# Two token halves of 320 in a diffusion step: PSUM slots by half, panels A A B B around norms, w_ada loaded with a later panel

## The chip, the cores and the metric
The kernel runs on one core of a Trainium2 chip. The metric is device time in microseconds (us) of one execution of the whole program. TensorE (PE) multiplies, VectorE (DVE) and ScalarE (ACT) work on vectors, GpSimd (POOL) helps with some of the weights, and SyncE (SP) issues the weight transfers.

## The reference
Two layers of a hybrid backbone run over 128 context and 512 latent tokens of width 1024, together 640 tokens with the same weights. The core of a layer is:

```python
n = rmsnorm(h, norm_g[l, 0]) * (1 + sc0) + s0
h = h + 0.5 * g0 * swiglu(n, w_ffn_up[l, 0], w_ffn_down[l, 0])
n = rmsnorm(h, norm_g[l, 1]) * (1 + sc1) + s1
y, ckv, k_r = token_mix(n, ...)
h = h + g1 * y
n = rmsnorm(h, norm_g[l, 2]) * (1 + sc2) + s2
h = h + 0.5 * g2 * swiglu(n, w_ffn_up[l, 1], w_ffn_down[l, 1])
```

All nine modulation vectors (s, sc, g) of a layer are c @ w_ada + b_ada: context and latent tokens have vectors of their own. The hidden width of swiglu is 2816. token_mix is one input product, a long convolution, attention, a Fourier mix, three gated branches and an output product. After the last layer comes a final rmsnorm.

## The kernel before
**Data.** Activations lie transposed: h is [128, 8, 640], eight blocks of 128 channels with all 640 tokens beside each other. A float32 product is made of three products of rounded halves: weights hi times input hi, hi times lo, and lo times hi. The tokens are cut into two halves of TH = 320. The second half has 192 latent and 128 context tokens; since modulation differs between the two kinds, an operation with a per-channel scalar is two instructions there.

**Panels.** Weights come as panels of 1 MB (two output tiles of 128 columns by 8 blocks of 128 rows; the last down projections of an FFN have 6 blocks). Each layer has 34 panels for an FFN (up 8, down 4, up 8, down 4, up 6, down 4), then 6 mix, 10 table, 4 head, 16 gate and 4 output panels, and again 34. There are SLOTS = 3 buffers. SP loads a panel into raw when PE has finished the panel three before it (`freed`), ACT rounds it to whi (round_panel, L734), DVE subtracts to wlo (split_panel, L1034). Both do so for the panel two ahead of the one PE is on, at a fixed place in their orders.

**PE.** `gemm` (L345) makes one output tile of all 640 tokens: it takes one of the two PSUM slots of tile_psum (two banks, one per half), runs 8 blocks x 2 inputs x 2 halves with whi (L355) and then 8 blocks x 2 halves with wlo (L360). A slot may be taken again when ACT or DVE has counted it free. An up panel holds a gate tile and an up tile.

**FFN on the other engines.** ACT applies Silu to the gate tile (L789), DVE multiplies it with the up tile (hidden, L1176), ACT rounds it (x_hi, L793), DVE makes x_lo (L1059). For a down panel DVE adds each tile into h (L1153); in the last chunk ACT squares h and DVE sums the squares.

**Norm.** When all of h is updated, PE sums the squares per token with ten small matmuls (L385), ACT takes the root, DVE the reciprocal and a diagonal of it (L1072), PE spreads it over the partitions (L389, L390), and DVE and ACT make n_hi and n_lo block by block (L1083, L771, L1098). PE starts the next stage's first tile as blocks come.

**w_ada.** 144 tiles of 512 KB are multiplied with the conditioning rows by DVE, two instructions each (L1118, L1120), inside `ada_step`, which stands behind each split_panel and takes as many tiles as ADA_PLAN says for the panel. 16 are done at the start. The rest have two buffers; DVE waits for a tile's transfer, SP's ada_load waits until DVE has used the tile two before. SP issues, in order, a panel load and then the w_ada tiles of the plan for the panel before it.

Every engine runs a fixed order written out in the program; the sequences of the listed functions are the order of work.

## Time and profile of the kernel before
| | us |
|---|---|
| median of 3 runs (lowest, highest) | 3858.5 (3857.25, 3859.94) |
| the profiled execution | 3861.88 |
| its span | 3860.1 |

| engine | busy us | share of the span |
|---|---|---|
| PE matmul | 3313.1 | 86% |
| PE weight load | 3140.2 | 81% |
| DVE | 1846.2 | 48% |
| ACT | 920.4 | 24% |
| POOL | 137.7 | 4% |

The mean granted clock of TensorE is 0.91 of 2.4 GHz. The core's transfers move 86 GB/s in the mean. Busy shares are means over stages. A wait is told with the engine and line that ended it; times in the timeline are from the start of the span. "L355" is line 355 of the kernel.

### The profile page before, as it was taken

The page shows a single profiled execution, that of the slowest core. Times are in us where ns is not written, and L with a number is a line of the kernel's source. Part 1 is how long each engine was busy: PE and PEld are TensorE (multiplying, and loading weights), DVE is VectorE, ACT ScalarE, POOL GpSimd, SP SyncE. Part 2 cuts the span into 40 slices and gives each one's busy share as a digit, 9 for nine tenths or more (in the row PEclk, how much of TensorE's full clock was granted, in tenths as well). Part 3 has the DMA queues.
Part 4 walks back from the last instruction along what each step waited for, and adds up shares of the span by engine and source line. Part 5 has one row for each costly group of instructions (what it writes and reads, how often), then busy time and mean ns, then how long its engine had stood idle before and what let it go on. Part 6 is the DMA issues. An engine that isn't in the chain of part 4 may idle for free.

```text
span 3860.1 us, 46383 instructions
## 1 busy us (share of the span) xinstructions
PE 3313.1 (86%) x20238; PEld 3140.2 (81%) x20238; DVE 1846.2 (48%) x2770; ACT 920.4 (24%) x1153; POOL 137.7 (4%) x100
## 2 busy tenths in 40 slices
PE   2998987766769998999979989796677799799998
PEld 2998987545659997999979989693466699799998
DVE  6445555567552244433454455646765333523223
ACT  2211112223331122111222111222233212321211
POOL 0000000221000000000000000001300000000000
PEclk9999998878779998999989999897876899899999
DMA  5333333110002122232323333230100222112221
GB/s 204 112 107 131 131 125 119 55 44 31 22 33 94 71 101 76 84 114 93 104 82 115 115 131 131 99 121 25 60 17 21 77 76 77 66 66 77 77 77 61
DMA packets 56891, 330.38 MB, mean 86 GB/s; under 512 B 6320, under 2 KB 6640, under 8 KB 29808
## 3 DMA queue, kind: packets, MB, share of 16 engines
q1 hardware_dynamic: 53280, 297.82, 21.6%
q10 hardware_dynamic: 3408, 29.60, 1.9%
q8 instruction: 159, 2.61, 0.3%
q14 instruction: 44, 0.36, 0.0%
HBM read 313.07 MB, written 14.32 MB: 85 GB/s over the span
## 4 chain that ended last, share of the span: by engine, by line
PE 66%; DVE 18%; DMA 6%; ACT 5%; issue 4%; SPq 0%; DVEq 0%; ACTq 0%
PE tile_psum L355 37%; PE tile_psum L360 19%; PE tile_psum L323 3%; DMA raw<-in_w_up 3%; PE misc_psum L530 2%; DVE scaled L1118 2%; ACT whi L734 2%; DVE wlo L1034 2%; DMA raw<-in_w_down 1%; PE misc_psum L323 1%; DVE w_ada L1120 1%; DVE n_lo L1098 1%; PE misc_psum L494 1%; DVE probs_t_lo L1059 1%; DMA n_lo<-n_keep 1%
## 5 line engine op out<-in xcount | busy, mean ns | idle before, releaser
L355 PE MATMUL tile_psum<-n_hi,whi 128*128 128x320 f32 x4224 | 990.1, 316 | 86.1 <-DVE n_lo L1098 38.9
L355 PE MATMUL tile_psum<-n_lo,whi 128*128 128x320 f32 x4224 | 980.6, 314 | 0.0
L355 PEld LDWEIGHTS tile_psum<-n_hi,whi 128*128 128x128 f32 x4224 | 718.9, 192 | 107.7 <-issue 63.2
L734 ACT ACTIVATE whi<-raw 128x2048 fp32r<-128x2048 f32 (+2 forms) x216 | 398.8, 1847 | 1466.7 <-PE tile_psum L360 945.4
L355 PEld LDWEIGHTS tile_psum<-n_lo,whi 128*128 128x128 f32 x4224 | 724.3, 192 | 0.0
L360 PE MATMUL tile_psum<-n_hi,wlo 128*128 128x320 f32 x4224 | 670.9, 311 | 0.0
L360 PEld LDWEIGHTS tile_psum<-n_hi,wlo 128*128 128x128 f32 x4224 | 639.9, 191 | 0.0
L1034 DVE TENSOR_TENSOR wlo<-raw,whi 128x2048 fp32r<-128x2048 f32 (+1 forms) x188 | 421.3, 2241 | 288.8 <-ACT whi L734 288.6
L355 PE MATMUL tile_psum<-x_hi,whi 128*128 128x320 f32 x1664 | 386.9, 314 | 59.4 <-DVE x_lo L1059 47.8
L355 PE MATMUL tile_psum<-x_lo,whi 128*128 128x320 f32 x1664 | 384.6, 313 | 0.0
L355 PEld LDWEIGHTS tile_psum<-x_hi,whi 128*128 128x128 f32 x1664 | 283.7, 192 | 62.7 <-DVE x_lo L1059 49.3
L1176 DVE TENSOR_TENSOR hidden<-gate_act,tile_psum 128x640 f32<-128x640 f32 x88 | 72.2, 820 | 477.1 <-PE tile_psum L360 475.1
L355 PEld LDWEIGHTS tile_psum<-x_lo,whi 128*128 128x128 f32 x1664 | 284.1, 192 | 0.0
L360 PE MATMUL tile_psum<-x_hi,wlo 128*128 128x320 f32 x1664 | 272.7, 313 | 0.0
L360 PEld LDWEIGHTS tile_psum<-x_hi,wlo 128*128 128x128 f32 x1664 | 255.5, 192 | 0.0
L717 POOL TENSOR_TENSOR wlo<-raw,whi 128x512 fp32r<-128x512 f32 x96 | 137.5, 1462 | 2760.1 <-ACT whi L734 2760.1
L1153 DVE SCALAR_TENSOR_TENSOR h<-tile_psum,ada_t,h 128x320 f32<-128x320 f32 x336 | 126.9, 433 | 205.9 <-PE tile_psum L360 204.5
L1059 DVE TENSOR_TENSOR x_lo<-hidden,x_hi 128x640 fp32r<-128x640 f32 x88 | 72.6, 825 | 308.3 <-ACT x_hi L793 308.3
L1118 DVE SCALAR_TENSOR_TENSOR scaled<-w_ada,c_rows 128x1024 f32<-128x1024 f32 x128 | 156.1, 1219 | 0.3
L1120 DVE SCALAR_TENSOR_TENSOR w_ada<-w_ada,c_rows 128x1024 f32<-128x1024 f32 x128 | 156.1, 1220 | 0.0
L789 ACT ACTIVATE gate_act<-tile_psum 128x640 f32<-128x640 f32 x88 | 61.7, 701 | 298.6 <-PE tile_psum L360 298.5
L1064 DVE TENSOR_TENSOR sq_sum<-sq_sum,squares 128x640 f32<-128x640 f32 x56 | 46.0, 822 | 139.0 <-ACT squares L754 139.0
(232 smaller groups left out, 2863.3 us busy)
## 6 DMA issues: line engine op xcount, KB each, us to landing
raw<-in_w_up SPq DMA_DIRECT2D x88, 1024.0 KB, 4.8
w_ada<-in_w_ada SPq DMA_DIRECT2D x128, 512.0 KB, 3.4
raw<-in_w_down SPq DMA_DIRECT2D x32, 1024.0 KB, 4.9
raw<-in_w_gate SPq DMA_DIRECT2D x32, 1024.0 KB, 4.8
raw<-in_tables SPq DMA_DIRECT2D x20, 1024.0 KB, 4.8
raw<-in_w_down SPq DMA_DIRECT2D x16, 768.0 KB, 4.4
raw<-in_w_mix SPq DMA_DIRECT2D x12, 1024.0 KB, 4.9
w_ada_early<-in_w_ada SPq DMA_DIRECT2D x16, 512.0 KB, 19.5
```

The lines of the kernel that those rows point to most:

```text
L323: ins = pe.matmul(o, w[a], x_[b], start=first and n == 0, stop=last and n == 2)
L355: pe.matmul(tps[:, t.s, j, 0:TH], blk(p, b0 + k)[0], x_[b], start=k == 0 and b == 0, stop=False)
L360: ins = pe.matmul(tps[:, t.s, j, 0:TH], blk(p, b0 + k)[1], x_[0], start=False, stop=k == n - 1)
L530: ins = pe.matmul(out, w[:, s, t * 512 + f * P:t * 512 + (f + 1) * P], x_[:, t, col:col + 512], start=b == 0 and t == 0 and x_ is tmh, sto ...
L717: ins = pool.tensor_tensor(wlo[:, s, a:b], raw[:, s, a:b], whi[:, s, a:b].bitcast(F32), ALU.subtract)
L734: act.activation(whi[:, r, 0:cols], raw[:, r, 0:cols], ACT.Copy).then_inc(hi_ready, 1)
L1034: dve.tensor_tensor(wlo[:, r, 0:cols], raw[:, r, 0:cols], whi[:, r, 0:cols].bitcast(F32), ALU.subtract)\
L1059: dve.tensor_tensor(out, src, hi.bitcast(F32), ALU.subtract).then_inc(ready, 1)
L1118: dve.scalar_tensor_tensor(out=junk, in0=w, scalar=1.0, in1=cb[:, 0, :], op0=ALU.mult, op1=ALU.mult, accum_out=ada[:, t, 0:1]).then_inc(ad ...
L1120: dve.scalar_tensor_tensor(out=w, in0=w, scalar=1.0, in1=cb[:, 1, :], op0=ALU.mult, op1=ALU.mult, accum_out=ada[:, t, 1:2]).then_inc(ada_u ...
L1153: ins = dve.scalar_tensor_tensor(out=hs, in0=tps[:, t.s, bank, c0:c1], scalar=ada[:, l * ADA_TILES + 8 * section + m, g:g + 1], in1=hs, op ...
L1176: dve.tensor_tensor(halves(hf[:, i % 2, :]), halves(sg[:, i % 2, :]), tile2(t), ALU.mult).then_inc(t.free, 1)
```

## The change
Each PSUM slot now holds the two output tiles of a panel (banks m = 0, 1) for one half of the tokens. `pair` (in place of `gemm` in the FFNs, the first two mix panels and the output panels) makes the (panel i, half j) unit; `walk` gives the order of units: for each panel half A then half B, but in the first two panels after a norm and the last two before it both A units and then both B units. A panel is freed by its B unit. `turn_of` gives the units behind which ACT and DVE round and split the next panel and DVE takes its w_ada tiles: the A unit of each panel (the B unit of the second panel behind a norm).

A norm is done per half. PE's sums for half A stand in the middle of the second last unit of the stage (token_sums(0)), its spread behind it, now as a product of the broadcast reciprocal with the identity, without DVE's diagonal. Half B's stand in the first unit of the next stage. DVE and ACT make five blocks of half A behind unit (n-2, B) and three behind the last unit; half B in two lots of four around the next stage's first unit.

ADA_PLAN is a list with one number per panel. SP's load of panel p waits for panel p-3, issues the panel, and then the w_ada tiles of the plan for panel p-3. Before, they were those of the plan for panel p-1. The output is stored in 16 pieces rather than 8, by half.

The diff, cut to its core. Removed lines of the functions printed above are left out in the engines' parts:

```diff
@@ -68,6 +68,8 @@
 SM_C, SM_S, SM_CI, SM_SI, SM_BD, SM_FC, SM_FS, NSM = 0, 128, 256, 384, 512, 768, 896, 1024
+HALVES = [[(0, TH, 0)], [(TH, TL, 0), (TL, T, 1)]]
+TOKEN_COLS = [(0, 0), (P, 0), (TH - P, TH - 2 * P)]
 SEGMENTS = [(0, 0, TH, 0, TH, 0), (1, 0, TL - TH, TH, TL, 0), (1, TL - TH, TH, TL, T, 1)]
...
 WIDTH = {"heads": 7 * P, "down6": 12 * P}
 ADA_EARLY = 16
-ADA_PLAN = [{"up0": 1, "down0": 1, "up1": 2, "down1": 2, "up2": 2, "down2": 1},
-            {"up0": 1, "down0": 0, "up1": 1, "down1": 0, "up2": 1, "down2": 1}]
+ADA_PLAN = [[0, 0, 2, 2, 1, 1, 1, 1] + [1] * 4 + [2] * 8 + [1] * 4 + [2] * 6 + [2, 2, 0, 0],
+            [0, 0, 2, 2, 1, 1, 1, 1] + [0] * 4 + [1] * 8 + [0] * 4 + [1] * 6 + [1, 1, 0, 0]]
+ADA_STEP = (ADA_PLAN[0] + [0] * (len(LAYER_KINDS) - 2 * len(FFN_KINDS)) + ADA_PLAN[1]) * DEPTH
+def walk(n, first=False, last=False):
+    steps = [(i, j) for i in range(n) for j in range(2)]
+    if first:
+        steps[:4] = [(0, 0), (1, 0), (0, 1), (1, 1)]
+    if last:
+        steps[-4:] = [(n - 2, 0), (n - 1, 0), (n - 2, 1), (n - 1, 1)]
+    return steps
+def turn_of(n, first=False, last=False):
+    return [(i, 1 if first and i == 1 else 0) for i in range(n - last)]
...
@@ tensor engine @@
+            held, norms_open = {}, {}
+            def pair(i, j, n, hi, lo, each=None, mid=None):
+                if j == 0:
+                    held[i] = panel_hi()
+                p = held[i]
+                t = taken(slots.tile())
+                tok = slice(j * TH, (j + 1) * TH)
+                for k in range(n):
+                    if each is not None:
+                        pe.wait_ge(*each(k))
+                    for b in range(2):
+                        for m in range(2):
+                            pe.matmul(tps[:, t.s, m, 0:TH], blk(p, m * n + k)[0], (hi, lo)[b][:, k, tok], start=k == 0 and b == 0, stop=False)
+                if j == 0:
+                    panel_lo(p)
+                if mid is not None:
+                    mid()
+                for k in range(n):
+                    for m in range(2):
+                        ins = pe.matmul(tps[:, t.s, m, 0:TH], blk(p, m * n + k)[1], hi[:, k, tok], start=False, stop=k == n - 1)
+                ins.then_inc(t.done, 1)
+                if j == 1:
+                    freed[p] = (t.done, t.done_at)
+            def token_sums(j):
+                norms_open[j] = m = taken(slots.misc())
                 pe.wait_ge(sum_ready, due(sum_ready))
+                for c, (a, _) in enumerate(TOKEN_COLS):
+                    ins = pe.matmul(mps[:, m.s, 0, 2 * c:2 * c + 2], acc[:, j * TH + a:j * TH + a + P], ones[:, 0:2], start=True, stop=True)
+                ins.then_inc(sums_done, 1)
+            def spread(j):
+                m = norms_open[j]
+                pe.wait_ge(inv_ready, due(inv_ready))
+                for c, (a, skip) in enumerate(TOKEN_COLS):
+                    ins = pe.matmul(mps[:, m.s, 1, a + skip:a + P], rr[:, 3 * j + c:3 * j + c + 1].broadcast_to([P, P]),
+                                    ident[:, skip:P], start=True, stop=True)
+                ins.then_inc(m.done, 1)
+            def from_norm():
+                now = due.now(n_ready)
+                due(n_ready, 2 * KT)
+                return lambda j: lambda k: (n_ready, now + KT * j + k + 1)
+            def begin(steps, coming, opened, n, hi, lo):
+                for i, j in steps[:4]:
+                    late = (i, j) == (0, 0) and not opened
+                    pair(i, j, n, hi, lo, coming(j) if i == 0 else None, (lambda: token_sums(1)) if late else None)
+                    if late:
+                        spread(1)
+            def end(steps, n, hi, lo, norm_next):
+                for i, j in steps[-4:]:
+                    early = norm_next and (i, j) == (steps[-1][0] - 1, 1)
+                    pair(i, j, n, hi, lo, None, (lambda: token_sums(0)) if early else None)
+                    if early:
+                        spread(0)
+            def ffn(opened=False):
+                coming_n = from_norm()
                 for c, n in enumerate(CHUNKS):
+                    steps = walk(n, first=c == 0)
+                    now = due.now(hid_ready)
+                    due(hid_ready, 2 * n)
+                    if c == 0:
+                        begin(steps, coming_n, opened, KT, nh, nl)
+                    for i, j in steps[4 if c == 0 else 0:]:
+                        pair(i, j, KT, nh, nl)
+                    down = walk(4, last=c == 2)
+                    for i, j in down[:4] if c == 2 else down:
+                        pair(i, j, n, xh, xl, (lambda k: (hid_ready, now + steps.index((k, j)) + 1)) if i == 0 else None)
+                    if c == 2:
+                        end(down, n, xh, xl, True)
...
@@ sync @@
+            def load(src):
+                p = at[0]
+                at[0] += 1
+                s, cols = p % SLOTS, WIDTH.get(KINDS[p], PANEL)
+                if p >= SLOTS:
+                    sp.wait_ge(*freed[p - SLOTS])
+                sp.dma_start(raw[:, s, 0:cols], src).then_inc(loaded[s], 16)
+                if p >= SLOTS:
+                    ada_load(ADA_STEP[p - SLOTS])
...
@@ scalar @@
+            def into_h(last=None):
+                turns = turn_of(4, last=last is not None)
+                for i, j in walk(4, last=last is not None):
+                    t = slots.tile()
                     if last:
+                        squares_of(i, j, t)
+                    if (i, j) in turns:
+                        round_panel()
+                    if last and (i, j) == (3, 0):
+                        token_root(0)
+                    if last and (i, j) == (2, 1) and last[0] < DEPTH:
+                        norm_hi(*last, 0, range(5))
+                    if last and (i, j) == (3, 1) and last[0] < DEPTH:
+                        norm_hi(*last, 0, range(5, KT))
+                        round_panel()
+                        token_root(1)
+            def ffn(f, norm, last):
                 for c, n in enumerate(CHUNKS):
+                    for i, j in walk(n, first=c == 0):
+                        first = c == 0 and (i, j) == (0, 0)
+                        if first:
+                            norm_hi(*norm, 1, range(4))
                         t = tile()
+                        tok = slice(j * TH, (j + 1) * TH)
+                        act.activation(sg[:, i % 2, tok], tps[:, t.s, 0, 0:TH], ACT.Silu).then_inc(sg_out, 1)
                         act.wait_ge(t.free, t.free_at)
+                        act.activation(xh[:, i, tok], hf[:, i % 2, tok], ACT.Copy).then_inc(hid_hi, 1)
+                        if first:
+                            norm_hi(*norm, 1, range(4, KT))
+                        if (i, j) in turn_of(n, first=c == 0):
+                            round_panel()
+                    into_h(last if c == 2 else None)
...
@@ vector @@
+            def open_norm(j):
                 m = slots.misc()
                 dve.wait_ge(rms_out, due(rms_out))
+                dve.reciprocal(rr[:, 3 * j:3 * j + 3], rs[:, 3 * j:3 * j + 3]).then_inc(inv_ready, 1)
+                due(inv_ready)
+                return m
+            def normalise(layer, i, j, m, ks):
+                def scale(k):
+                    if len(norm_made) >= 4:
+                        dve.wait_ge(n_ready, norm_made[-4])
+                    norm_made.append(due(n_ready))
+                    out = scaled[(len(norm_made) - 1) % 4]
+                    for a, b, g in HALVES[j]:
+                        at = slice(a - j * TH, b - j * TH)
+                        ins = dve.scalar_tensor_tensor(out=out[:, at], in0=h[:, k, a:b], scalar=gm[:, 8 * i + k, g:g + 1],
+                                                       in1=mps[:, m.s, 1, at], op0=ALU.mult, op1=ALU.mult)
                     ins.then_inc(t_ready, 1)
+                    return out, due(t_ready)
+                if ks[0] == 0:
+                    seen(m)
+                coming = [scale(ks[0])]
+                for k in ks:
+                    if k != ks[-1]:
+                        coming.append(scale(k + 1))
+                    t, made = coming.pop(0)
+                    dve.wait_ge(t_ready, made)
                     if k + 1 == KT:
                         dve.sem_inc(m.free, 1)
                     dve.wait_ge(hi_out, due(hi_out))
+                    for a, b, g in HALVES[j]:
+                        ins = dve.scalar_tensor_tensor(out=nl[:, k, a:b], in0=t[:, a - j * TH:b - j * TH],
+                                                       scalar=ada[:, layer * ADA_TILES + 24 * i + k, g:g + 1],
                                                        in1=nh[:, k, a:b].bitcast(F32), op0=ALU.add, op1=ALU.subtract)
                     ins.then_inc(n_ready, 1)
...
+            def sum_squares(i, j):
+                tok = slice(j * TH, (j + 1) * TH)
+                dve.wait_ge(sq_out, due(sq_out, 2))
+                if i == 0:
+                    own(dve.tensor_tensor(acc[:, tok], sq_half[0], sq_half[1], ALU.add))
+                else:
+                    for m in range(2):
+                        own(dve.tensor_tensor(acc[:, tok], acc[:, tok], sq_half[m], ALU.add))
+                if i == 3:
+                    dve.sem_inc(sum_ready, 1)
+            def into_h(section, plan, last=None):
+                turns = turn_of(4, last=last is not None)
+                for i, j in walk(4, last=last is not None):
                     t = tile()
+                    for m in range(2):
+                        for a, b, g in HALVES[j]:
+                            hs = h[:, 2 * i + m, a:b]
+                            at = slice(a - j * TH, b - j * TH)
+                            ins = dve.scalar_tensor_tensor(out=hs, in0=tps[:, t.s, m, at],
+                                                           scalar=ada[:, l * ADA_TILES + 8 * section + 2 * i + m, g:g + 1],
+                                                           in1=hs, op0=ALU.mult, op1=ALU.add)
                     ins.then_inc(t.free, 1)
+                    dve.wait_ge(t.free, t.free_at)
+                    if last:
+                        sum_squares(i, j)
+                    if (i, j) in turns:
                         split_panel()
+                        ada_step(plan[i])
+                    if last and (i, j) == (3, 0):
+                        m0 = open_norm(0)
+                    if last and (i, j) == (2, 1) and last[0] < DEPTH:
+                        normalise(*last, 0, m0, range(5))
+                    if last and (i, j) == (3, 1) and last[0] < DEPTH:
+                        normalise(*last, 0, m0, range(5, KT))
+                        m1 = open_norm(1)
+                        split_panel()
+                        return m1
+                    if last and (i, j) == (2, 1) and last[0] == DEPTH:
+                        finish(0, m0)
+            def ffn(f, norm, m1, last):
+                plan = ADA_PLAN[f]
                 for c, n in enumerate(CHUNKS):
+                    for i, j in walk(n, first=c == 0):
+                        first = c == 0 and (i, j) == (0, 0)
+                        if first:
+                            normalise(*norm, 1, m1, range(4))
                         t = tile()
+                        tok = slice(j * TH, (j + 1) * TH)
+                        dve.wait_ge(sg_out, due(sg_out))
+                        dve.tensor_tensor(hf[:, i % 2, tok], sg[:, i % 2, tok], tps[:, t.s, 1, 0:TH], ALU.mult).then_inc(t.free, 1)
                         dve.wait_ge(t.free, t.free_at)
+                        lo_part(xl[:, i, tok], hf[:, i % 2, tok], xh[:, i, tok], hid_ready, hid_hi)
+                        if first:
+                            normalise(*norm, 1, m1, range(4, KT))
+                        if (i, j) in turn_of(n, first=c == 0):
+                            if f == 1 and c == 0 and i == 2:
+                                dve.wait_ge(c_back, due(c_back, 16))
+                            split_panel()
+                            ada_step(plan[i])
+                    m1 = into_h(2 if f == 0 else 8, plan[n:], last if c == 2 else None)
+                    plan = plan[n + 4:]
+                return m1
...
```

## Rows read from the trace of the kernel before

**Rows 1.** PE's waits of the whole span: who waited, us in total, times, longest.
```profile
PE misc_psum L385 <- DVEq L1165: 43.5, 6, 7.8
```

**Rows 2.** PE's timeline, a norm of layer 0: start us, us, instruction, idle before.
```profile
1463.40 2.26 PE L385 MATMUL misc_psum<-constants,sq_sum 128*128 128x2 f32 x10 [7.76 <-DVEq L1165]
...
1495.31 2.51 PE L360 MATMUL tile_psum<-n_hi,wlo 128*128 128x320 f32 x16
```

**Rows 3.** The same timeline at the other ends and beginnings of stages.
```profile
73.96 0.87 PE L355 MATMUL tile_psum<-n_hi,whi 128*128 128x320 f32 x2 [3.35 <-DVE n_lo L1098]
...
96.06 2.51 PE L360 MATMUL tile_psum<-n_hi,wlo 128*128 128x320 f32 x16
103.11 2.51 PE L360 MATMUL tile_psum<-n_hi,wlo 128*128 128x320 f32 x16
...
601.87 2.26 PE L385 MATMUL misc_psum<-constants,sq_sum 128*128 128x2 f32 x10 [7.75 <-DVEq L1165]
...
1963.77 2.27 PE L385 MATMUL misc_psum<-constants,sq_sum 128*128 128x2 f32 x10 [7.75 <-DVEq L1165]
...
1996.31 2.51 PE L360 MATMUL tile_psum<-n_hi,wlo 128*128 128x320 f32 x16
...
2496.91 2.26 PE L385 MATMUL misc_psum<-constants,sq_sum 128*128 128x2 f32 x10 [7.76 <-DVEq L1165]
...
3354.61 2.26 PE L385 MATMUL misc_psum<-constants,sq_sum 128*128 128x2 f32 x10 [7.76 <-DVEq L1165]
...
3386.42 2.51 PE L360 MATMUL tile_psum<-n_hi,wlo 128*128 128x320 f32 x16
...
3844.62 2.08 PE L385 MATMUL misc_psum<-constants,sq_sum 128*128 128x2 f32 x10 [4.66 <-DVEq L1165]
```

**Rows 4.** SP's queue in two stretches, and the transfer issued at 1456.04 (last: us to landing).
```profile
293.16 2.62 SPq L665 DMA_DIRECT2D w_ada<-in_w_ada  x2
295.83 0.43 SPq L650 DMA_DIRECT2D raw<-in_w_up  x1
...
1455.66 0.33 SPq L650 DMA_DIRECT2D raw<-in_w_up  x1
1456.04 0.43 SPq L665 DMA_DIRECT2D w_ada<-in_w_ada  x1
...
w_ada<-in_w_ada SPq DMA_DIRECT2D x1, 512.0 KB, 5.7
```

**Rows 5.** DVE's timeline: scaling at a norm, a w_ada tile, the final scaling.
```profile
70.64 1.92 DVE L1083 SCALAR_TENSOR_TENSOR scaled<-h,norm_scale,misc_psum 128x512 f32<-128x512 f32 x4 [2.66 <-PE misc_psum L390]
...
342.03 1.22 DVE L1118 SCALAR_TENSOR_TENSOR scaled<-w_ada,c_rows 128x1024 f32<-128x1024 f32 x1
...
344.32 0.81 DVE L1176 TENSOR_TENSOR hidden<-gate_act,tile_psum 128x640 f32<-128x640 f32 x1
...
3850.74 6.42 DVE L1466 SCALAR_TENSOR_TENSOR h<-h,constants,misc_psum 128x640 f32<-128x640 f32 x8 [2.66 <-PE misc_psum L390]
```

**Rows 6.** PE's timeline, products with a new weight block at every matmul.
```profile
708.83 0.28 PE L323 MATMUL misc_psum<-small_hi,fnet_in_lo 128*128 128x256 f32 x1
708.94 0.28 PE L323 MATMUL misc_psum<-small_hi,fnet_in_hi 128*128 128x256 f32 x1
```

**Rows 7.** DVE's timeline, an update of h by three pieces.
```profile
1946.53 1.14 DVE L1153 SCALAR_TENSOR_TENSOR h<-tile_psum,ada_t,h 128x320 f32<-128x320 f32 x3
```

**Rows 8.** PE after gaps: three of the timeline, then two of the chain of waits.
```profile
514.96 0.54 PE L355 MATMUL tile_psum<-n_hi,whi 128*128 128x320 f32 x2 [2.62 <-ACT gate_act L789]
...
585.81 0.90 PE L355 MATMUL tile_psum<-x_hi,whi 128*128 128x320 f32 x2 [3.78 <-DVE h L1153]
...
1397.58 0.87 PE L355 MATMUL tile_psum<-n_hi,whi 128*128 128x320 f32 x2 [5.22 <-DVE n_lo L1059]
...
585.81 6.53 PE tile_psum L355 x24
...
1397.58 6.43 PE tile_psum L355 x32
```

More of the change, by code:

```diff
@@ L212, in program @@
         ident, ones, eps = cst("ident"), cst("ones"), cst("eps")
-        diag = tn[:, 1, :]
+        scaled = [tn[:, b // 2, b % 2 * TH:(b % 2 + 1) * TH] for b in range(4)]
+        sq_half = [sq[:, b * TH:(b + 1) * TH] for b in range(2)]
         junk = tn[:, :, :].rearrange("p a t -> p (a t)")[:, 0:D]
@@ L629, in _ @@
                 n_coming = coming(n_ready, KT)
-                for i in range(4):
-                    p = panel_hi()
-                    gemm(p, 0, nh, nl, 0, KT, n_coming if i == 0 else None, True)
-                    gemm(p, KT, nh, nl, 0, KT)
+                outs = walk(4, last=True)
+                for i, j in outs[:4]:
+                    pair(i, j, KT, nh, nl, n_coming if (i, j) == (0, 0) else None)
+                end(outs, KT, nh, nl, True)
                 ffn()
-            inverse_rms()
+            token_sums(1)
+            spread(1)
         @block.sync
@@ L775, in into_h @@
-            def into_h(last):
-                for i in range(4):
-                    t = [slots.tile(), tile()]
-                    round_panel()
-                    if last:
-                        for j in range(2):
-                            square(2 * i + j, t[j])
-            def ffn(f):
-                norm(2 * f)
+                act.wait_ge(sums_done, due(sums_done))
+                m = (slots.miscs - 1) % 2
+                act.activation(rs[:, 3 * j:3 * j + 3], mps[:, m, 0, 0:6:2], ACT.Sqrt, bias=eps, scale=1.0 / D).then_inc(rms_out, 1)
@@ L818, in _ @@
             round_panel()
+            token_root(0)
+            token_root(1)
             round_panel()
+            norm_hi(0, 0, 0, range(KT))
             for l in range(DEPTH):
-                ffn(0)
-                norm(1)
+                ffn(0, (l, 0), (l, 1))
+                norm_hi(l, 1, 1, range(4))
+                t = tile()
+                for c in range(2):
+                    split_hi(fnh[:, c, 0:TH], tps[:, t.s, c, 0:TH])
+                norm_hi(l, 1, 1, range(4, KT))
+                round_panel()
                 act.wait_ge(n_ready, due.now(n_ready))
@@ L828, in _ @@
                 act.dma_start(ft[:, :], feats).then_inc(feat_in, 16)
+                t10 = tile()
                 for c in range(2):
[L830 to L836 removed]
+                    for bank, c0, c1, t0, t1, g in SEGMENTS[:1]:
+                        act.activation(upad[:, c, t0 + 1:t1 + 1], tps[:, t10.s, c, c0:c1], ACT.Copy).then_inc(t10.free if c else conv_in, 1)
+                t = tile()
+                for c in range(2):
+                    split_hi(fnh[:, c, TH:T], tps[:, t.s, c, 0:TH])
+                t = tile()
+                for c in range(2):
+                    for bank, c0, c1, t0, t1, g in SEGMENTS[1:]:
+                        ins = act.activation(upad[:, c, t0 + 1 + 2 * g:t1 + 1 + 2 * g], tps[:, t.s, c, c0:c1], ACT.Copy)
+                        ins.then_inc(t.free if g and c else conv_in, 1)
+                round_panel()
+                for c in range(2, 6):
+                    t = tile()
+                    act.wait_ge(conv_used, due(conv_used))
                     for bank, c0, c1, t0, t1, g in SEGMENTS:
@@ L1198, in _, with fnet_lo @@
             split_panel()
+            m0, m1 = open_norm(0), open_norm(1)
             split_panel()
+            normalise(0, 0, 0, m0, range(KT))
             for l in range(DEPTH):
-                ffn(0)
+                m1 = ffn(0, (l, 0), m1, (l, 1))
                 dve.wait_ge(par_in, due(par_in, 16))
-                norm(1)
-                for c in range(2):
+                def fnet_lo(j):
                     t = tile()
-                    lo_part(halves(fnl[:, c, :]), tile2(t), halves(fnh[:, c, :]), t.free)
+                    tok = slice(j * TH, (j + 1) * TH)
+                    dve.wait_ge(op_hi, due(op_hi, 2))
+                    for c in range(2):
+                        ins = dve.tensor_tensor(fnl[:, c, tok], tps[:, t.s, c, 0:TH], fnh[:, c, tok].bitcast(F32), ALU.subtract)
+                    ins.then_inc(t.free, 1)
+                normalise(l, 1, 1, m1, range(4))
+                fnet_lo(0)
+                normalise(l, 1, 1, m1, range(4, KT))
                 split_panel()
+                t10 = slots.tile()
+                fnet_lo(1)
+                t11 = slots.tile()
                 for c in (0, UP - 1, TL + 1, TL + 2):
```

185 lines of the change are left out of this document (53 added, 132 removed).

## The prediction, made before the changed kernel ran
> **What bounds the kernel now.** I read the page's busy table first: TensorE (PE) works through most of the span. That is a share of the whole; the waits decide what a change of order can give, so the second view is PE's waits by releaser, where the sums before each norm stand high [rows 1]. Then I read PE's timeline at a norm and measured the loss against undisturbed work. The reader is to see in it where one stage's last matmul ends and from where the next stage's tiles follow each other evenly. One PSUM tile of 8 blocks takes 7.04 us (103.11 less 96.06, [rows 3]): 48 matmuls at 0.147 us. A tile of 6 blocks has 36, so 5.28 us.
>
> At the norm of layer 0 before its second FFN the old stage's last matmul ends at 1463.40 - 7.76 = 1455.64. The low pass of the second new tile should start 7.04 + 4.69 us later (32 of its 48 matmuls stand ahead of it), at 1467.4; it starts at 1495.31, so the norm costs 27.9 us [rows 2]. The same subtraction gives 27.8 for the last such norm [rows 3] and 28.3 to 28.6 for the other three (1963.77 and 1996.31 belong to one): 141 us in five.
>
> Inside the FFNs the same ruler gives the rest. An FFN is 22 up and 12 down panels, two tiles each: 60 x 7.04 + 8 x 5.28 = 464.6 us. From the second tile's low pass (96.06, so the stage's start would be 84.33) to the end of layer 0's first FFN (601.87 - 7.75 = 594.12) it is 45.2 us more than that; layer 1's first FFN 40.0; the second FFNs 7.8 and 0.7 [rows 2, 3]. Sum 93.7. The first FFNs lose because SP's queue loads a panel only after two w_ada tiles: at 293.16 it issues them in 2.62 us, and the panel at 295.83 [rows 4]. Those w_ada issues wait for VectorE (DVE), which waits for the previous panel: a ring that runs slower than PE's 14.08 us a panel.
>
> **The change, norms.** Panels run A A B B about a norm, so half A is summed, spread and mostly scaled under the last B tiles, and half B under the next stage's A tiles. What is left on the path, per norm: (1) DVE comes late to the last B tile, since it has five blocks of half A to scale behind the tile before. Today a block of 640 columns costs DVE about 1.9 us (four pieces in 1.92 us scale two blocks, [rows 5], and as much again makes their low parts), a half about 1. After the last B tile come two h updates, the squares, and blocks 5 to 7: about 8.7 us, where PE wants block 7 after 4.1, so 4.5 late. (2) PE's own small matmuls, twice: today 2.26 us for ten of two columns [rows 2], so 0.7 for three, and about 0.8 for the spread, an estimate; 3.0 for both halves. (3) 1.3 for the clock after such a wait. Together 8.8 of 28.2, a saving of 19.4, five times: 97. Bounds: 25 if only the small matmuls stay, 12 if half A is scaled wholly behind the last tile; 60 to 125 in all. At the start the first tile begins at 73.96, so the second's low pass would be due at 85.69 and comes at 96.06 [rows 3]; most of these 10.4 us go, and the diagonal that DVE makes first: 10 saved, 5 to 13. At the end 20.1 us lie behind the last matmul (3844.62 - 4.66 to 3860.1), 6.42 of them the scaling of h [rows 5]; half A's share of that, of the sums and of the stores goes ahead of it: 8 saved, 5 to 10. Sum 115.
>
> **The change, PE's order.** Each matmul now takes another weight block than the one before; today two to four in a row share one. The nearest row with a change at every matmul is the 128x256 product in the Fourier branch, 0.11 us from start to start [rows 6], where 256 columns at 2.4 GHz are 0.107; so a block is in place within 0.11 us, and the 0.147 of 320 columns cover it. Today's high pass (a change every four) and low pass (every two) go at one pace. I take 0. The other end, from that row: 0.01 each over some 13,000 matmuls, 130 us; below nothing it can't be, since 0.133 of the 0.147 are the columns.
>
> **The change, w_ada.** This is the term that decides. SP now issues, behind the load of panel k+3, the w_ada tiles that DVE consumes in its turn k. The load of panel k+3 waits until PE has finished panel k, that is its B tile; call that moment F. But DVE's turn k now stands behind the A tile of panel k, 7 us before F. DVE is in order, so it stands in ada_tiles with the B tile of panel k unread, and PE cannot start the B tile of panel k+1, which has the same PSUM slot. Queued behind the wait on DVE: the hidden product or h updates of the B tile, its low part, the next split. For them wait ScalarE (x_hi, after the slot is free) and PE.
>
> When does the tile land? Today, too, some w_ada loads stand right behind a panel: panel at 1455.66, w_ada at 1456.04, landed 5.7 us later [rows 4]; six such pairs in all land between 5.6 and 5.9. So F + 0.03 + 0.37 + 5.7 = F + 6.1. A w_ada tile costs DVE 2.3 us (342.03 to 344.32, where the hidden product follows, [rows 5]), a second one has landed by the time the first is done. Then the hidden product of 320 columns, 0.45 (0.81 for 640), and PE starts: F + 8.95. It was due at F + 6.85 (a next tile starts 0.19 before the semaphore of the last one). With 0.1 for the restart, an up panel with one w_ada tile loses 2.2 us, with two 4.5. A down panel has four h pieces instead (three take 1.14, [rows 7]; I take 1.3, an estimate): 3.0. A down panel of 6 blocks, whose A tile ends 1.76 earlier: 7.0 with two, 4.7 with one.
>
> The Trainium skill ("DMA: Bandwidth & Descriptors", Anatomy of one DMA) fits a transfer as about 2.0 us plus its bytes over 436 GB/s; the 1.5 MB of panel and tile together would by that, an estimate, be in at F + 5.6, and each loss would be 0.5 us smaller. The trace's 5.7 after the second issue is what I use.
>
> Counts from ADA_PLAN: first FFN: 4 up panels with one, 16 with two, 8 down with one, 2 small down with two: 8.8 + 72 + 24 + 14 = 118.8. Second FFN of layer 0: 18 up with one, 2 with two, 2 small down with one: 39.6 + 9 + 9.4 = 58. In layer 1 it has only the last 8 tiles: 17.8. Sum 2 x 118.8 + 58 + 17.8 = 313. It replaces the 93.7 of today, because the old ring (panel behind w_ada on SP) is indeed undone: +219 us. Bounds: at least 0 (no wait, below), at most 313 with none of the old loss gone.
>
> **The clock.** In the FFNs, after gaps of 2.62 us and less PE goes on at 2.4 GHz. After 3.78 us it ran 24 matmuls in 6.53 us instead of 3.5, after 5.22 us 32 in 6.43 instead of 4.7: the 1.2 GHz level for part of them, costing 3.0 and 1.7 us [rows 8]. The gaps of the 40 panels with two tiles are 4.5 us (4 of them 7), each just ahead of a B tile, which is on the path. Bounds 0 and 3.0 each; I take 1.7, since 4.5 lies between both and some may pass: 68 us. The Trainium skill ("TensorE: Matmul & The Clock Gate", HAM oscillation) describes a kernel whose transfer wait in every tile brings the half clock back in every tile; by that rule all 40 pay, and with 3.0 each it would be 120. The rows above agree as far as single gaps go.
>
> **Sum.** The profiled execution took 3861.9 (span 3860.1), 3.4 above the median of the runs, 3858.5. 3861.9 - 115 + 219 + 68 = 4034 us.
>
> **Rivals.**
> (a) DVE never waits for w_ada. It would need DVE to reach its turn k over 6.1 us after F, 13 us behind the tile that releases it. For it: DVE is busy less than half the time and 12 us stalls show that it can be late. Against: with no wait before it DVE reaches its turn within 5 us (0.45 of product, its low part, a split of 2.3). Then both savings stand: 3861.9 - 115 - 94 = 3653, faster. This is also what comes out if the norms' gain were all that counted.
> (b) The wait comes as computed, but the gaps leave the clock alone: 3966.
> (c) Every gap with two tiles costs 3.0, the 16 down gaps of 3.0 us cost 1.7 each, and the norms save 20 less: 3966 + 147 + 20 = 4133. The changing weights, if they cost at all, lead here too.
> (d) The norms swallow all: saving 60 in place of 97, otherwise as forecast: 4071, inside the range.
>
> **Chances.** Forecast with (d) 0.64, (b) 0.19, (c) 0.08, (a) 0.07, something that evens out 0.02. Range 3945 to 4115; the likeliest case alone has 3985 to 4085. A change under 0.2% (8 us) could not be told from none. Faster 0.08, same 0.01, slower 0.91.
>
> **What will show it.** DVE's scaled<-w_ada should have idle time before it, released by the w_ada transfer, some 10 us in each of 88 panels; PE should wait before its B tiles in FFNs, for hidden and h; the panel pitch should be 16.3 (one tile) and 18.6 to 21 (two) in the first FFNs. SP should no longer wait for w_ada's consumption. At norms PE's idle time should fall from 28 to under 10 us. Granted clock in the first FFNs should be below today's. If DVE shows no wait for w_ada, the forecast is wrong in its main term.

## The result, and the profile after

The changed kernel takes 4120.6 us (4116.2 to 4128.9, four runs) beside 3859.0 (3857.3 to 3859.9) for the kernel before: a ratio of 1.0678, with a 95% interval of 1.0665 to 1.0691. It is slower, as forecast, but 87 us more so than the 4034 predicted and 5.6 above the end of the range. Its profiled execution took 4128.9 us, with a span of 4127.1 beside 3860.1.

The page of the changed kernel: its span, the busy time of each engine, and the chain that ended last by engine.

```profile
span 4127.1 us, 47341 instructions
PE 3400.4 (82%) x20308; PEld 3228.8 (78%) x20308; DVE 1887.3 (46%) x3084; ACT 966.3 (23%) x1436; POOL 138.2 (3%) x100
PE 58%; DVE 19%; DMA 14%; issue 4%; ACT 4%; SPq 1%; DVEq 0%; ACTq 0%
```

Before, DMA was 6% of the chain and PE 66%. Nothing larger is being moved: the bytes are the same to 0.1 MB. A transfer has come onto the path, and the waits say which (engine, tile and line, what it waited for; then us in total, times, longest).

```profile
DVE scaled L1251 <- DMA w_ada<-in_w_ada: 807.8, 91, 11.8
PE tile_psum L413 <- DVE hidden L1331: 232.4, 67, 5.7
PE tile_psum L413 <- DVE h L1299: 84.5, 22, 7.4
PE tile_psum L413 <- DVE n_lo L1223: 25.1, 17, 4.2
```

DVE stands 808 us in 91 waits for w_ada, and PE waits behind it for the two things that DVE makes from PSUM, hidden and h: 317 us (232.4 and 84.5). The wait for the sums before a norm, 43.5 us before [rows 1], is down to 4.7 us in two waits.

One panel with two w_ada tiles, on three engines. SP's timeline (start, duration, line, what it issues):

```profile
301.48 0.33 SPq L744 DMA_DIRECT2D raw<-in_w_up  x1
301.85 0.91 SPq L735 DMA_DIRECT2D w_ada<-in_w_ada  x2
322.34 0.33 SPq L744 DMA_DIRECT2D raw<-in_w_up  x1
```

DVE's timeline (the bracket is idle time before it and what ended it):

```profile
307.51 1.22 DVE L1251 SCALAR_TENSOR_TENSOR scaled<-w_ada,c_rows 128x1024 f32<-128x1024 f32 x1 [10.97 <-DMA w_ada<-in_w_ada]
...
309.81 1.22 DVE L1251 SCALAR_TENSOR_TENSOR scaled<-w_ada,c_rows 128x1024 f32<-128x1024 f32 x1
...
312.10 0.48 DVE L1331 TENSOR_TENSOR hidden<-gate_act,tile_psum 128x320 f32<-128x320 f32 x1
...
328.37 1.23 DVE L1251 SCALAR_TENSOR_TENSOR scaled<-w_ada,c_rows 128x1024 f32<-128x1024 f32 x1 [9.66 <-DMA w_ada<-in_w_ada]
```

PE's timeline:

```profile
305.98 2.51 PE L420 MATMUL tile_psum<-n_hi,wlo 128*128 128x320 f32 x16
...
312.64 0.90 PE L413 MATMUL tile_psum<-n_hi,whi 128*128 128x320 f32 x2 [4.15 <-DVE hidden L1331]
313.34 0.74 PE L413 MATMUL tile_psum<-n_lo,whi 128*128 128x320 f32 x2
...
319.80 2.51 PE L420 MATMUL tile_psum<-n_hi,wlo 128*128 128x320 f32 x16
```

Read it in a circle. PE ends a panel and frees its buffer, so SP issues the next load at 301.48 and w_ada at 301.85. It lands at 307.51, 5.66 later. Its products and those of the second w_ada tile occupy DVE to 312.10; the hidden product of the B tile, which PE finished at 301.45, follows, and PE may begin at 312.64 after 4.15 us of nothing. The pair of matmuls then takes 0.90 and 0.74 rather than 0.46: the 1.2 GHz level. The panel's pitch, 322.34 less 301.48, is 20.86 us, where 14.08 are work. SP no longer waits for w_ada anywhere in these FFNs, as it did before [rows 4]. The windows of the second and third chunk of layer 0's first FFN (stretch, its length, busy time and count of PE, PEld, DVE, ACT, POOL, granted clock, DMA share, GB/s), after:

```profile
289.00:700.00 411.00, 319.12 (x1874) 313.92 (x1875) 173.99 (x280) 62.64 (x87) 0.00 (x0) 0.87 0.25 95
```

and before:

```profile
257.00:592.00 335.00, 300.01 (x1979) 297.07 (x1979) 182.18 (x269) 60.09 (x55) 0.00 (x0) 0.95 0.35 128
```

PE is busy 78% of the time at a granted clock of 0.87; before it was 90% at 0.95.

The norm of layer 0 before its second FFN, the answer to [rows 2], on PE's timeline:

```profile
1540.32 2.51 PE L420 MATMUL tile_psum<-n_hi,wlo 128*128 128x320 f32 x16
...
1547.36 0.72 PE L430 MATMUL misc_psum<-constants,sq_sum 128*128 128x2 f32 x6
1547.95 2.60 PE L420 MATMUL tile_psum<-n_hi,wlo 128*128 128x320 f32 x16
1550.38 0.78 PE L438 MATMUL misc_psum<-constants,inv_rms 128*128 128x128 f32 x6
...
1555.75 2.51 PE L420 MATMUL tile_psum<-n_hi,wlo 128*128 128x320 f32 x16
...
1564.37 0.90 PE L413 MATMUL tile_psum<-n_hi,whi 128*128 128x320 f32 x2 [3.18 <-DVE n_lo L1223]
...
1568.08 2.59 PE L420 MATMUL tile_psum<-n_hi,wlo 128*128 128x320 f32 x16
...
1575.88 2.50 PE L420 MATMUL tile_psum<-n_hi,wlo 128*128 128x320 f32 x16
...
1586.29 3.14 PE L420 MATMUL tile_psum<-n_hi,wlo 128*128 128x320 f32 x16
...
1593.96 2.51 PE L420 MATMUL tile_psum<-n_hi,wlo 128*128 128x320 f32 x16
...
1601.00 2.51 PE L420 MATMUL tile_psum<-n_hi,wlo 128*128 128x320 f32 x16
```

Each low pass closes a tile. Seven tiles lie between the first and the last row and take 60.68 us where 7 x 7.04 = 49.28 are work, so this norm costs 11.4 us instead of 27.9. Most of the gain that the halves were to bring is there: the five norms cost 11.0, 11.4, 15.5, 12.8 and 14.3, together 65 instead of 141.

The same subtraction over the whole trace, loss beyond undisturbed work, forecast and measured, in us. Gap is PE's idle time before a B tile, restart the 0.27 us that a tile at full speed loses besides it, clock what is lost beyond both:

```
                                           forecast  measured
start of the first FFN                        -10      -12
five norms                                    -97      -76
mix stages                                      0       -2
end                                            -8       -4
old loss in the FFNs gone                     -94      -94
48 panels with one w_ada tile, gap+restart   +123     +138
 the same, clock                                0      +43
40 panels with two, gap+restart              +190     +202
 the same, clock                              +68      +72
sum                                          +172     +267
```

Each is rounded by itself. The two spans differ by 267.0.

### The profile page after: what moved, and what is told of

Its sections match the earlier page's. It is cut to its first block, busy times and chain, and to the rows that moved or that the text cites. A ratio compares the mean times of both kernels' runs of the same rounds, so it can differ in the third digit from the quotient of the medians.

```text
span 4127.1 us, 47341 instructions
## 1 busy us (share of the span) xinstructions
PE 3400.4 (82%) x20308; PEld 3228.8 (78%) x20308; DVE 1887.3 (46%) x3084; ACT 966.3 (23%) x1436; POOL 138.2 (3%) x100
## 3 DMA queue, kind: packets, MB, share of 16 engines
q8 instruction: 160, 2.62, 0.3%
## 4 chain that ended last, share of the span: by engine, by line
PE 58%; DVE 19%; DMA 14%; issue 4%; ACT 4%; SPq 1%; DVEq 0%; ACTq 0%
PE tile_psum L413 24%; DMA w_ada<-in_w_ada 13%; PE tile_psum L420 11%; PE tile_psum L374 9%; PE tile_psum L379 5%; DVE scaled L1251 3%; PE tile_psum L342 3%; DVE w_ada L1253 3%; PE misc_psum L608 2%; PE misc_psum L342 1%; DVE h L1299 1%; PE misc_psum L572 1%; DVE probs_t_lo L1179 1%; DVE scaled L1206 1%; DVE hidden L1331 1%
## 5 line engine op out<-in xcount | busy, mean ns | idle before, releaser
L413 PE MATMUL tile_psum<-n_hi,whi 128*128 128x320 f32 x3200 | 797.3, 333 | 245.2 <-DVE hidden L1331 197.2
L413 PEld LDWEIGHTS tile_psum<-n_lo,whi 128*128 128x128 f32 x3200 | 586.5, 205 | 0.0
L1251 DVE SCALAR_TENSOR_TENSOR scaled<-w_ada,c_rows 128x1024 f32<-128x1024 f32 x128 | 156.6, 1224 | 807.8 <-DMA w_ada<-in_w_ada 807.8
L420 PE MATMUL tile_psum<-n_hi,wlo 128*128 128x320 f32 x3200 | 508.7, 312 | 0.0
L420 PEld LDWEIGHTS tile_psum<-n_hi,wlo 128*128 128x128 f32 x3200 | 484.1, 191 | 0.0
L413 PE MATMUL tile_psum<-x_lo,whi 128*128 128x320 f32 x1408 | 339.6, 324 | 0.0
L892 ACT ACTIVATE x_hi<-hidden 128x320 fp32r<-128x320 f32 x176 | 82.9, 471 | 748.9 <-DVE hidden L1331 748.9
L374 PE MATMUL tile_psum<-n_hi,whi 128*128 128x320 f32 x1024 | 237.6, 313 | 24.2 <-DMA n_lo<-n_keep 24.2
L420 PE MATMUL tile_psum<-x_hi,wlo 128*128 128x320 f32 x1408 | 222.4, 309 | 0.0
L890 ACT ACTIVATE gate_act<-tile_psum 128x320 f32<-128x320 f32 x176 | 75.8, 431 | 615.4 <-PE tile_psum L420 615.2
L420 PEld LDWEIGHTS tile_psum<-x_hi,wlo 128*128 128x128 f32 x1408 | 210.4, 188 | 0.0
L1299 DVE SCALAR_TENSOR_TENSOR h<-tile_psum,ada_t,h 128x320 f32<-128x320 f32 (+1 forms) x336 | 126.8, 433 | 181.1 <-PE tile_psum L420 180.1
```

What stands on the lines that cost most here:

```text
L374: pe.matmul(tps[:, t.s, j, 0:TH], blk(p, b0 + k)[0], x_[b], start=k == 0 and b == 0, stop=False)
L413: pe.matmul(tps[:, t.s, m, 0:TH], blk(p, m * n + k)[0], (hi, lo)[b][:, k, tok], start=k == 0 and b == 0, stop=False)
L420: ins = pe.matmul(tps[:, t.s, m, 0:TH], blk(p, m * n + k)[1], hi[:, k, tok], start=False, stop=k == n - 1)
L892: act.activation(xh[:, i, tok], hf[:, i % 2, tok], ACT.Copy).then_inc(hid_hi, 1)
L1251: dve.scalar_tensor_tensor(out=junk, in0=w, scalar=1.0, in1=cb[:, 0, :], op0=ALU.mult, op1=ALU.mult, accum_out=ada[:, t, 0:1]).then_inc(ad ...
L1299: ins = dve.scalar_tensor_tensor(out=hs, in0=tps[:, t.s, m, at], scalar=ada[:, l * ADA_TILES + 8 * section + 2 * i + m, g:g + 1], in1=hs, ...
```

## The experiments

The kernel before took 3857.8 and 3858.3 us beside them. The first three move one thing each in the changed kernel.

**w_ada two panels later instead of three.**

```diff
-                if p >= SLOTS:
-                    ada_load(ADA_STEP[p - SLOTS])
+                if p >= 2:
+                    ada_load(ADA_STEP[p - 2])
```

> The changed kernel with one edit: SP issues the w_ada tiles of DVE's turn k behind the load of panel k+2 instead of k+3, one panel (14 us) sooner. Theory: the FFN loss of the changed kernel comes from DVE waiting for w_ada ahead of the B tile. The tiles then land about 1 us before the turn, so DVE's wait on them falls from 808 us to under 50, the 455 us lost in the FFNs to under 20, and the gain at norms and ends stays: about 3680 us. Rival 1, the work by halves itself (slots by half, twice the instructions and handshakes) makes PE wait for hidden and h: stays above 4000. Rival 2, the pair of panel and tile issued back to back is what comes late: as the changed kernel, 4120, since the pair is still issued together.

3684.1 us (3682.4 to 3687.5), ratio to the kernel before 0.9548 (0.9534 to 0.9562). SP, DVE and PE in its trace, for a panel with two tiles:

```profile
282.90 0.33 SPq L744 DMA_DIRECT2D raw<-in_w_up  x1
283.85 2.62 SPq L735 DMA_DIRECT2D w_ada<-in_w_ada  x2
```

```profile
293.31 2.29 DVE L1154 TENSOR_TENSOR wlo<-raw,whi 128x2048 fp32r<-128x2048 f32 x1 [1.24 <-ACT whi L811]
295.52 1.22 DVE L1251 SCALAR_TENSOR_TENSOR scaled<-w_ada,c_rows 128x1024 f32<-128x1024 f32 x1
...
300.11 0.48 DVE L1331 TENSOR_TENSOR hidden<-gate_act,tile_psum 128x320 f32<-128x320 f32 x1
```

```profile
301.48 2.51 PE L420 MATMUL tile_psum<-n_hi,wlo 128*128 128x320 f32 x16
...
308.52 2.51 PE L420 MATMUL tile_psum<-n_hi,wlo 128*128 128x320 f32 x16
...
315.56 2.51 PE L420 MATMUL tile_psum<-n_hi,wlo 128*128 128x320 f32 x16
```

The first tile is issued 11.7 us before DVE takes it, there is no idle time before it, and PE's low passes follow each other in 7.04. The wait of DVE for w_ada is gone from the waits, and PE's for hidden and h are 6 us together instead of 317. One index in SP's list is worth 436 us, 11% of the kernel. The pair of issues occupies SP for 2.62 us here and for 0.91 in the changed kernel: SP now waits for DVE to use the tile two before, up to 2.2 us at a time, and with the loads so early nothing is late for it.

```profile
SPq L735 <- DVE w_ada L1253: 83.8, 67, 2.2
```

**w_ada one panel later.** The same edit with 1.

> The changed kernel with the w_ada tiles of turn k issued behind the load of panel k+1, as in the kernel before. Theory: DVE never waits for w_ada, but SP waits for DVE again before it may load the next panel, in the panels with two tiles. By its steps that ring runs at 14.4 us a panel in this order, against 16.4 in the kernel before, since the turn stands behind the A tile, half a panel sooner: 10 to 20 us above the run with k+2, about 3690. If the ring costs what it did before, 3680 + 90 = 3770.

3703.0 us (3697.1 to 3706.6), 0.9599 (0.9583 to 0.9615), 13 above the figure named. SP's waits:

```profile
SPq L735 <- DVE w_ada L1253: 605.0, 104, 14.8
```

The ring of the old kernel is back on the queue: SP stands in the w_ada issue until DVE has freed a buffer, and the next panel load stands behind it. In the new order this version is 19 us slower than the one two later, not more, so the ring was never a reason to go as far as three.

**The turn behind the B tile.** w_ada stays three panels later; ScalarE and DVE take their turn behind each panel's B tile instead of its A tile, but for the second last panel of a stage, where it stays behind the A tile.

```diff
-    return [(i, 1 if first and i == 1 else 0) for i in range(n - last)]
+    return [(i, 0 if last and i == n - 2 else 1) for i in range(n - last)]
```

> The changed kernel with w_ada behind panel k+3 as it is, but the turn (round and split of the next panel, w_ada tiles) behind the B unit of each panel instead of the A unit (third panel from the stage's end as it is). Theory: DVE reads the B tile, frees its slot and only then waits for w_ada, from about F+5 to F+6.1, and is through by F+10.7, before the next B tile ends: PE does not wait. Near 3685 us, DVE's wait for w_ada about 1 us a turn, under 150 in all. If it is the late tile itself that costs, whatever stands behind it, the time stays above 4000.

3703.3 us (3699.4 to 3708.2), 0.9597 (0.9583 to 0.9612), some 18 above the figure named. DVE's wait for w_ada, 807.8 in the changed kernel:

```profile
DVE scaled L1251 <- DMA w_ada<-in_w_ada: 94.4, 84, 5.2
```

It still waits 84 times, about 1 us each, but one tile later in the order, where nothing that PE needs at once is queued behind it. So what costs is neither the late load nor the early turn but the two together. Late transfers alone do not hurt: 84 waits remain in a kernel 4% faster than before. What it is slower by than the version two later, 19 us, lies at the ends of the first three FFNs, their norms included, and in the mix stages; the cause stays open.

**The old kernel with w_ada three later.** The counts of ADA_PLAN are laid out by panel, and the loads stand behind panel p for turn p-3; all else is the kernel before.

```diff
                 sp.dma_start(raw[:, s, 0:cols], src).then_inc(loaded[s], 16)
+                if p >= SLOTS:
+                    ada_load(ADA_STEP[p - SLOTS])
...
-                        ada_load(step)
```

> The kernel before with one edit: SP issues the w_ada tiles of DVE's turn k behind the load of panel k+3, as the change does. In the old order the turn stands behind both tiles of panel k. Theory: this edit is good by itself; SP's ring goes, DVE waits about 1 us a turn behind work that nobody needs, and the 94 us lost in the FFNs fall to some 10, with up to 3 more at the norms: 3770 to 3785. Rival: w_ada three panels later costs in any order: 4000 or more.

3776.2 us (3772.9 to 3777.9), 0.9785 (0.977 to 0.9799). With it the square is complete:

```
                         w_ada with panel +1   +2     +3
panels as before                3858            -    3776
halves, A A B B at norms        3703          3684    4121
```

Each part by itself is a gain. Three later takes 82 us off the old kernel, where DVE's turn stands behind both tiles. The halves alone, with w_ada one later as before, take 155. Between the best of each row the halves are worth 92 (3776 to 3684), and the rows of norms, start, mix stages and end above say 95. Together as they were made, the two lose 262.

**PE kept busy in the gaps.** To price the clock by itself: the changed kernel, with matmuls into an unused PSUM bank where PE would stand, 26 where two tiles are awaited and 12 where one is, not in an FFN's first chunk nor in the last FFN. Their product is not used.

```diff
...
+                for _ in range(fill):
+                    pe.matmul(mps[:, 0, 0, 0:TH], blk(p, 0)[0], hi[:, 0, 0:TH], start=True, stop=True)
...
```

> The changed kernel as it is, waits included, but PE runs matmuls whose result nobody reads (into the idle misc_psum) in the time in which it would stand before a B tile: 26 of 320 columns (3.8 us) where two w_ada tiles are awaited, 12 (1.8 us) where one, in the second and third chunk of the first FFNs and of layer 0's second FFN. This sorts the FFN loss into waiting and clock. Theory: B tiles lost 6.5 us behind two tiles, 4.5 of it waiting, and about 3 behind one, 2.3 of it waiting; the rest is the 1.2 GHz level after each gap. With PE busy until 0.7 us before the slot is free the level stays at 2.4 GHz, the wait itself stays: losses 4.7 and 2.3, in all 30 x 1.7 + 20 for the single ones = 70 us less, about 4050. Rival: what is beyond the wait is not the clock after idle time (a dearer restart, changing weight blocks): 4120, or above by what the extra matmuls overrun.

4050.1 us (4041.3 to 4057.5), 1.0496 (1.0476 to 1.0515). Its window over the same stretch, which here reaches 24 us into the mix stage, and its PE timeline:

```profile
289.00:700.00 411.00, 382.50 (x2540) 376.19 (x2541) 199.48 (x335) 79.67 (x118) 0.00 (x0) 0.98 0.27 100
```

```profile
415.75 3.97 PE L407 MATMUL misc_psum<-n_hi,whi 128*128 128x320 f32 x26
...
420.15 0.56 PE L415 MATMUL tile_psum<-n_hi,whi 128*128 128x320 f32 x2 [0.43 <-DVE hidden L1344]
```

The granted clock is 0.98 instead of 0.87, and the B tile begins at full speed. 70 us come back by useless work: the 30 filled panels with two tiles lose 4.9 us on average instead of 6.8, the 25 with one 2.9 instead of 3.9. Four of these 55 still met the 1.2 GHz level, behind 2.2 to 2.6 us of idle time that the filling left. The clock's share of the whole loss is thus at least 70; the table above puts it at 115, and 33 panels with a tile have no filling.

**What the norms still hold.** Built on the version two later. First, all eight blocks of half A are scaled in one piece behind the second last B tile, instead of five and three around the last one's h update:

```diff
...
-                        norm_hi(*last, 0, range(5))
+                        norm_hi(*last, 0, range(KT))
...
```

> On the kernel with w_ada behind panel k+2 (3684 us): DVE and ACT make all eight blocks of half A behind the second last tile of a stage, where it was five and three. Theory of the norm loss (65 us in five, 12 to 13 each): PE starts the new stage at once and stands 3.2 us before block 5, then runs at 1.2 GHz for a while, 2 more. With eight blocks ahead, blocks come in time, but the last B tile is read 2.8 us later and so the sums of half B, in the middle of the first new tile, wait some 2 us instead: 5.3 becomes about 2.5, 10 to 15 us less in all, 3670. Rival: the wait only moves from the blocks to the sums and the clock falls as before: 3680 to 3685.

3677.1 us (3673.3 to 3678.9), 0.9527 (0.9511 to 0.9543): 7 less, between the two figures. Then also half B one tile later: its sums ahead of the second A tile, its spread in the middle, and DVE reads the first A tile before it scales half B.

> The same and PE takes half B's sums behind the first new A tile and its spread in the middle of the second; DVE and ACT read the first A tile before they make half B's blocks, all eight in one lot. By the steps of the trace: sums ready 2 us before PE asks, half B's blocks from 1.2 us each, the last one 3.5 us after PE could use it, in short waits that leave the clock alone: 7 us a norm where it is 12 to 13, 25 to 30 us less than 3684, about 3657. Rival: half B's blocks come too late and each wait brings the 1.2 GHz level: 3680 or more.

3667.3 us (3663.2 to 3671.1), 0.9504 (0.949 to 0.9519), the fastest kernel measured, 5.0% below the kernel before, though 10 above the figure named. PE around the same norm:

```profile
1366.33 2.51 PE L420 MATMUL tile_psum<-n_hi,wlo 128*128 128x320 f32 x16
...
1373.95 2.60 PE L420 MATMUL tile_psum<-n_hi,wlo 128*128 128x320 f32 x16
...
1381.76 2.51 PE L420 MATMUL tile_psum<-n_hi,wlo 128*128 128x320 f32 x16
...
1388.80 2.50 PE L420 MATMUL tile_psum<-n_hi,wlo 128*128 128x320 f32 x16
...
1397.30 2.59 PE L420 MATMUL tile_psum<-n_hi,wlo 128*128 128x320 f32 x16
...
1401.00 0.56 PE L413 MATMUL tile_psum<-n_hi,whi 128*128 128x320 f32 x2 [0.26 <-DVE n_lo L1221]
...
1402.17 0.57 PE L413 MATMUL tile_psum<-n_hi,whi 128*128 128x320 f32 x2 [0.32 <-DVE n_lo L1221]
...
1408.47 2.51 PE L420 MATMUL tile_psum<-n_hi,wlo 128*128 128x320 f32 x16
...
1416.39 2.51 PE L420 MATMUL tile_psum<-n_hi,wlo 128*128 128x320 f32 x16
```

Six tiles lie between the first and the last row: 50.06 us for 42.24 of work, 7.8 lost, 3.6 fewer than the 11.4 of the changed kernel. Five norms make 18, and 16.8 are measured. The gap of 3.18 and its slow clock are gone; what is left is 4.1 us in the tile that begins with half B's blocks, which come every 1.17 us (1402.17 less 1401.00) where PE's first pass wants one every 0.59, four matmuls.

## Why the prediction was off

**The mechanism held.** It named the wait that decides, its place and its releaser. DVE waits for w_ada in nearly every one of the 88 panels with a tile (91 waits), PE before the B tiles, for hidden and h. It had the landing at F + 6.1 and PE's start for two tiles at F + 11.2: with F = 301.45, the end of PE's tile and just before SP's issue, the rows give 6.06 and 11.19. The Trainium skill's fit, which the prediction names beside this term ("DMA: Bandwidth & Descriptors", Anatomy of one DMA), is given there for transfers that GpSimd issues; these are SP's, and its estimate of F + 5.6 was too early. The gaps are 2.27 (one tile, 30 up panels) and 4.55 (two, 36) on average where it said 2.1 and 4.4 without the restart. SP's waits for w_ada went. Rival (a), that DVE never waits, fell: it would have been 3653, and the kernel whose loads are early enough for it took 3684.

**The step that failed: the clock after a gap with one tile.** The prediction put it at nothing, because "after gaps of 2.62 us and less PE goes on at 2.4 GHz" [rows 8]. In the changed kernel 24 of the 48 one-tile panels met the 1.2 GHz level, 43 us beyond the restart: 12 of the 32 with a gap of 1.85 to 2.74 us, at some 1.5 each, 11 of the 13 with 2.82 to 4.38, a stretch that [rows 8] had left empty up to 3.78, and the one with 4.98. Two gaps of the same length in PE's timeline, some 200 us apart:

```profile
1660.04 0.56 PE L413 MATMUL tile_psum<-n_hi,whi 128*128 128x320 f32 x2 [1.86 <-DVE hidden L1331]
...
1664.84 2.51 PE L420 MATMUL tile_psum<-n_hi,wlo 128*128 128x320 f32 x16
...
1866.97 0.56 PE L413 MATMUL tile_psum<-n_hi,whi 128*128 128x320 f32 x2 [1.85 <-DVE hidden L1331]
...
1867.73 0.73 PE L413 MATMUL tile_psum<-n_hi,whi 128*128 128x320 f32 x2
...
1873.30 2.51 PE L420 MATMUL tile_psum<-n_hi,wlo 128*128 128x320 f32 x16
```

From the gap's end to the low pass it is 4.80 us after the one and 6.33 after the other. Rival (c), 4133, came nearest in number, with 147 us more of clock loss than (b), at the two-tile gaps and the 16 down gaps, and 20 less from the norms. Of the clock 115 came, over all gaps; of the norms 21. That it came near is in part luck: its clock loss sat at other gaps, and it had no longer gaps or restarts. The error was in drawing a threshold from single gaps in a kernel where gaps are rare; here they return every 16 us. Why one gap pays and its neighbour doesn't stays open: no experiment varied the gap's length or place alone.

The 40 gaps with two tiles were sized well: 68 us forecast, 72 measured, all 40 at the slow level. The Trainium skill ("TensorE: Matmul & The Clock Gate", HAM oscillation) says that a transfer wait in every tile brings the half clock back in every tile; these 40 of 40 agree. In the filled kernel, at a clock of 0.98, the transfers come as late, so what counts is that PE stands idle in the wait. The waits of that page's kernel are about 3 to 5 us; most one-tile gaps here are shorter, and 24 of the 48 paid all the same.

**The small sizes in the FFNs.** Gap and restart cost 27 us more than forecast over 88 panels: 15 of these are the restart, 0.27 us each and not 0.1, 10 the gaps of the up panels, 2.27 where 2.1 was meant and 4.55 where 4.4 was, and the rest those of the down panels.

**The norms: 76 and not 97.** The step that said 8.8 us left per norm measured 13.0. Its parts for layer 0's second FFN (11.4): small matmuls, 0.6 for the sums and 0.8 for the spread of each half, 2.7 together, forecast 3.0. DVE late with block 5 of half A: 3.2 where 4.5 was said. The restart and the clock after it 1.5, where 1.3 was said. What was not there at all: 4.0 us in the first B tile, where DVE feeds half B's blocks slower than PE takes them, and the clock is at the lower level once more (its low pass takes 3.14, not 2.51). The prediction had considered half B hidden under the A tiles. The last experiment shows it as the part that remains. The start held (12, forecast 10). The end brought 4.5 where 8 was said, with 5 as the lower bound: 5.9 us fewer lie behind the last tile, but 1.4 of half A's small matmuls now stand among the last tiles.

**The alternating weight blocks** cost nothing, as taken: undisturbed tiles take 7.04 us in the kernels with halves as in the kernel before.

**The sum.** 95 us were missing (4128.9 of the profiled execution less 4034): FFNs 74 (43 the clock in one-tile panels, 27 gap and restart, 4 the clock at two-tile gaps), norms 21, start, mix stages and end nothing together. With 1.7 for every gap the same sum would have given 4034 + 82 = 4116, for a reason half right: fewer gaps paid, and the norms kept more.

## What to carry to other kernels

When a load is queued behind the event that also releases its consumer's neighbours, work out both times from one moment (here the end of a panel): the load lands 6.1 us after it, and DVE asks 4.9 before it, since its wait of 10.97 began at 296.54. Two edits that each gain alone (82 and 155 us) lost 262 together, because one moved a transfer later and the other moved its reader earlier on an in-order engine that has PSUM to empty; try such a pair apart, and shift the queue by one place before giving either up. And where a new wait comes back in every tile, price the clock for all of its gaps, short ones too.

## What the hardware showed that was not expected

- Gaps of PE as short as 1.85 us were followed by the 1.2 GHz level, at some 1.5 us each, in 12 of 32 cases between 1.85 and 2.74; others of the same length were not. Before, none at 2.62 us or below had been [rows 8].
- Useless matmuls in the gaps, 26 or 12 at a time, are worth more than they cost: the FFN's granted clock goes from 0.87 to 0.98, and the kernel from 4120.6 to 4050.1 us.
